# Two layers of a hybrid token mixer with mixture of experts: first norm of layer 1 inside the combination, second norms with paired squares, experts' order written before the row lists

## The reference

```
for l in range(2):
    hx = rms_norm(x, norm1_g[l]) * (1 + scx1) + shx1        # first norm; context likewise
    ... px = hx @ w_in[l]; three mixers ...
    x = x + gx1 * merge_branches(...)
    h2 = rms_norm(x, norm2_g[l]) * (1 + scx2) + shx2        # second norm
    x = x + gx2 * moe_ffn(h2, router, experts, shared)
# rms_norm(z, g) = z * rsqrt(mean(z*z) + 1e-6) * g
# moe_ffn: scores = sigmoid(h @ w_router); the 8 best experts of the 4 best groups of 8;
#   y = 2.5 * sum over them of gate * (silu(h@Wg[e]) * (h@Wu[e])) @ Wd[e]  +  shared(h)
```

## Time and profile before

| | |
|---|---|
| three runs, us | 2924.26, 2929.12, 2937.09; median 2929.12 |
| the profiled execution, us | 2925.09 |
| its span, us | 2923.3 |
| TensorE's mean granted clock (1 is full) | 0.929 |
| busy: TensorE, its weight loads, VectorE, ScalarE, GpSimd | 85%, 56%, 44%, 27%, 16% |
| moved by DMA | 462 MB |

### The profile page before, as it was taken

One profiled execution on the slowest core, in us unless ns is written; L12 is line 12 of the kernel. 1 busy time (PEld: TensorE's weight loads), 2 busy tenths in 40 slices (PEclk: granted clock), 3 DMA queues, 4 the chain that ended last, 5 costly groups with the idle time before them and its releaser, 6 DMA issues. The chain is left out here.

```text
span 2923.3 us, 50391 instructions
## 1 busy us (share of the span) xinstructions
PE 2487.6 (85%) x20460; PEld 1627.9 (56%) x20460; DVE 1282.5 (44%) x2785; ACT 800.9 (27%) x1915; POOL 479.5 (16%) x530
## 2 busy tenths in 40 slices
PE   6999889588879997899898599988678879797976
PEld 3444455277744444466665455557367768664544
DVE  4877664787741013532222600054767741422213
ACT  2111264554430002122222101053445430121211
POOL 0000000244430001032232000000235420122220
PEclk8999999699989997999999799989699989899998
DMA  8646101000023201599895723113000033299885
GB/s 339 244 187 246 71 31 44 30 4 3 3 106 138 110 0 49 228 388 350 338 353 213 316 87 115 58 60 116 1 3 3 3 147 135 86 420 367 354 347 230
DMA packets 73831, 462.03 MB, mean 158 GB/s; under 512 B 19072, under 2 KB 26368, under 8 KB 44416
## 3 DMA queue, kind: packets, MB, share of 16 engines
q1 hardware_dynamic: 46848, 408.42, 35.4%
q0 software_dynamic: 26752, 50.39, 4.6%
HBM read 441.95 MB, written 62.91 MB: 173 GB/s over the span
## 5 line engine op out<-in xcount | busy, mean ns | idle before, releaser
L501 PE MATMUL win_ps<-h,win_ring 128*128 128x512 f32 (+1 forms) x1024 | 398.0, 550 | 18.6 <-PEq L377 13.2
L2315 PE MATMUL xp_psG<-moe_ring,rt_xt 128*64 128x256 f32 (+1 forms) x2048 | 351.8, 396 | 5.1 <-DMA moe_ring<-in_moe 4.8
L501 PEld LDWEIGHTS win_ps<-h,win_ring 128*128 128x128 f32 x1024 | 196.1, 193 | 211.9 <-issue 205.0
L2315 PEld LDWEIGHTS xp_psG<-moe_ring,rt_xt 128*64 128x64 f32 (+1 forms) x2048 | 255.8, 167 | 76.1 <-issue 19.1
L561 DVE SCALAR_TENSOR_TENSOR mod_acc<-ada_ring,cv_silu,mod_acc 128x512 f32<-128x512 f32 x280 | 198.0, 748 | 10.8 <-issue 0.4
L2336 PE MATMUL xp_psY<-moe_ring,rt_aT 128*64 128x512 f32 (+1 forms) x512 | 178.6, 606 | 13.8 <-DVE rt_aT L2587 13.8
L2198 POOL DMA_INDIRECT y_rows<-rt_y,rt_dst x92 | 92.3, 1004 | 495.7 <-DVE rt_y L2592 250.1
L1931 PE MATMUL mg_psG<-h,mg_ring 128*128 128x512 f32 (+1 forms) x480 | 166.7, 507 | 0.0
L2580 DVE TENSOR_TENSOR rt_sg<-rt_sg,xp_psG 128x128 f32<-128x128 f32 x92 | 26.4, 287 | 288.8 <-ACT rt_sg L2387 288.8
L1734 PE MATMUL sc_ps<-sc_NT,sc_XI 64*64 64x64 f32 x2560 | 149.0, 220 | 1.0
L2300 PEld LDWEIGHTS xp_psT<-cst,rt_xg 128*128 128x128 f32 x736 | 85.0, 145 | 111.5 <-DMA rt_xg<-h_rows,rt_tok 73.0
(11 more groups left out here) (448 smaller groups left out, 4199.2 us busy)
## 6 DMA issues: line engine op xcount, KB each, us to landing
moe_ring<-in_moe SPq DMA_DIRECT2D x128, 1536.0 KB, 13.0
ada_ring<-in_ada SPq DMA_DIRECT2D x22, 2048.0 KB, 14.9
win_ring<-in_win SPq DMA_DIRECT2D x20, 2048.0 KB, 7.8
cb_yg<-y_rows SPq DMA_DIRECT2D x24, 1024.0 KB, 15.5
mg_ring<-in_mg SPq DMA_DIRECT2D x10, 1536.0 KB, 7.7
mg_ring<-in_mg SPq DMA_DIRECT2D x16, 768.0 KB, 4.4
ml_gate_ring<-in_mg SPq DMA_DIRECT2D x18, 512.0 KB, 3.6
mg_wo<-in_wo SPq DMA_DIRECT2D x2, 4096.0 KB, 16.4
```

The lines of the kernel that those rows point to most:

```text
L501: last = pe.matmul(ps[:, n % NB, first(n):T], ring[:, j % 2, c, m * P:(m + 1) * P], h[:, c, first(n):T], start=c == 0, stop=c == KD - 1)
L2315: last = pe.matmul(psG[at:at + m, u % 2, 0:2 * P].rearrange("p (q n) -> p q n", q=2), xt[:, u % 2, c, at:at + m], ring[:, slot, c:2 * KD:K ...
```

## The change

1. **Second norms.** VectorE adds the squares in pairs, so that TensorE sums four tiles and not eight. The inverse root is exp(-0.5 ln(.)), both on ScalarE, with no reciprocal. VectorE makes scale and shift of the last two channel tiles itself. SP loads the router's weights here, in the stage ahead of the one that uses them.
2. **First norm of layer 1.** It is no longer a stage. stage_combine of layer 0 runs inside layer 1's frame and norms each tile of 128 tokens behind its residual: one square over 1024 columns, sums, logarithm, exponential, one multiplication over 1024 columns, eight modulations of 128. Half of the slots of `cb_yg` lie in `pr`. The projection's first weights are loaded behind the last rows, and `x` is written in two parts.
3. **Experts' order.** TensorE computes it behind 6 (layer 0) or 8 (layer 1) of the shared expert's first products, and VectorE writes `perm` and `passes` before the eight rounds of the row lists.

```diff
-def stage_norm(nc, k, l, which, x, h, t0, x_home=None):
-
-    sq_done, sum_done, root_done, scaled, h_done, x_saved = k.signals(
-        "norm_sq", "norm_sum", "norm_root", "norm_scaled", "norm_h", "norm_x_saved")
+def stage_norm(nc, k, l, x, h, t0, wr):
+
+    sq_done, pair_done, sum_done, logged, root_done, scaled, h_done = k.signals(
+        "norm_sq", "norm_pair", "norm_sum", "norm_log", "norm_root", "norm_scaled", "norm_h")
     N = T - t0
-    shift, scale = (0, 1) if which == 1 else (3, 4)
...
+
+            @block.sync
+            def _(sp):
+                sp.dma_start(wr[:], k.d_rt[l].rearrange("p (c n) -> p c n", n=E_ROUTED)).then_inc(k.wr_in.sem, 16)
...
                 act.wait_ge(sum_done.sem, sum_done.at(1))
-                act.activation(rstd[:, t0:T], ps[:, 0:N], ACT.Sqrt, scale=1.0 / D, bias=k.cst("eps")[:, 0:1]
-                               ).then_inc(root_done.sem, 1)
...
-                for c in range(KD):
+                act.activation(rstd[:, t0:T], ps[:, 0:N], ACT.Ln, scale=1.0 / D, bias=k.cst("eps")[:, 0:1]
+                               ).then_inc(logged.sem, 1)
+                act.wait_ge(logged.sem, logged.at(1))
+                act.activation(rstd[:, t0:T], rstd[:, t0:T], ACT.Exp, scale=-0.5).then_inc(root_done.sem, 1)
+                for c in range(KD - BY_DVE):
                     act.wait_ge(scaled.sem, scaled.at(c + 1))
-                    for s in range(2):
-                        if s * CTX >= t0:
-                            last = act.activation(h[:, c, s * CTX:(s + 1) * CTX], tmp[:, c, s * CTX:(s + 1) * CTX],
-                                                  ACT.Identity,
-                                                  scale=k.mod[:, l, s, scale * KD + c:scale * KD + c + 1],
-                                                  bias=k.mod[:, l, s, shift * KD + c:shift * KD + c + 1])
+                    for out, src, scale, shift in parts(c):
+                        last = act.activation(out, src, ACT.Identity, scale=scale, bias=shift)
                     last.then_inc(h_done.sem, 1)
...
             def _(dve):
+                for c in range(0, KD, 2):
+                    dve.wait_ge(sq_done.sem, sq_done.at(c + 2))
+                    dve.tensor_tensor(tmp[:, c, t0:T], tmp[:, c, t0:T], tmp[:, c + 1, t0:T], ALU.add
+                                      ).then_inc(pair_done.sem, 1)
                 dve.wait_ge(root_done.sem, root_done.at(1))
-                dve.reciprocal(rstd[:, t0:T], rstd[:, t0:T])
-                dve.drain()
...
+                dve.drain()
+                for c in range(KD - BY_DVE, KD):
+                    for out, src, scale, shift in parts(c):
+                        last = dve.tensor_scalar(out, src, scale, shift, ALU.mult, ALU.add)
+                    last.then_inc(h_done.sem, 1)
 
             @block.tensor
             def _(pe):
-                for c in range(KD):
-                    pe.wait_ge(sq_done.sem, sq_done.at(c + 1))
-                    last = pe.matmul(ps[:, 0:N], k.cst("ones"), tmp[:, c, t0:T], start=c == 0, stop=c == KD - 1)
+                for c in range(0, KD, 2):
+                    pe.wait_ge(pair_done.sem, pair_done.at(c // 2 + 1))
+                    last = pe.matmul(ps[:, 0:N], k.cst("ones"), tmp[:, c, t0:T], start=c == 0, stop=c == KD - 2)
                 last.then_inc(sum_done.sem, 1)
...
-                sp.dma_start(wr[:], k.d_rt[l].rearrange("p (c n) -> p c n", n=NE)).then_inc(wr_in.sem, 16)
                 sp.dma_start(sw, k.d_moe[l, E_ROUTED:E_ALL].rearrange("a p (c n) -> p a c n", n=P)
                              ).then_inc(sw_in.sem, 16)
...
-                for c in range(4, KD):
+                for c in range(4, KD if l else 6):
+                    shared_in(0, 0, c)
+                pe.wait_ge(ordered.sem, ordered.at(1))
+                pe.matmul(psOrder[:, 0:NE], eid[:], oh[0:NE], start=True, stop=True)
+                pe.matmul(psOrder[:, NE:NE + 4], k.cst("ones", NE)[:, 0:1], over[:], start=True, stop=True
+                          ).then_inc(order_ps.sem, 1)
+                for c in range(KD if l else 6, KD):
                     shared_in(0, 0, c)
                 for c in range(KD):
                     last = shared_in(0, 1, c)
                 last.then_inc(gu_done.sem, 1)
-                pe.wait_ge(ordered.sem, ordered.at(1))
-                pe.matmul(psOrder[:, 0:NE], eid[:], oh[0:NE], start=True, stop=True)
-                pe.matmul(psOrder[:, NE:NE + 4], k.cst("ones", NE)[:, 0:1], over[:], start=True, stop=True
-                          ).then_inc(order_ps.sem, 1)
...
                 windowed(1)
-                for j in range(HALF // 8):
-                    last = eight(j)
-                last.then_inc(listed.sem, 1)
...
+
+                for j in range(HALF // 8):
+                    last = eight(j)
+                last.then_inc(listed.sem, 1)
...
+
+            low = pr[:].rearrange("p a n -> p (a n)").rearrange("p (s j n) -> p s j n", j=PER, n=D)
+            yg += [low[:, j] for j in range(SL - own)]
+            sq = ctx.enter_context(nc.sbuf_tensor(f"cn_sq{l}", [P, 2, KD, P], F32))
+            tmp = ctx.enter_context(nc.sbuf_tensor(f"cn_tmp{l}", [P, 2, KD, P], F32))
+            rstd = ctx.enter_context(nc.sbuf_tensor(f"cn_rstd{l}", [P, 2, P], F32))
+            psN = ctx.enter_context(nc.psum_tensor(f"cn_ps{l}", [P, 2, 512], F32))
...
+                    sp.dma_start(yg[m % SL], d_y[m // NG, m % NG]).then_inc(y_in[m % SL].sem, 16)
+                if norm:
+                    load_projection(sp, k, l + 1, 0)
+                    load_projection(sp, k, l + 1, 1)
+                    for i, (a, b) in enumerate(((0, NTT - 1), (NTT - 1, NTT))):
+                        sp.wait_ge(x_done.sem, x_done.at(b))
+                        sp.dma_start(k.d_x[:, :, a * P:b * P], x[:, :, a * P:b * P]).then_inc(x_saved.sem, 16)
+                        sp.wait_ge(x_saved.sem, x_saved.at(16 * i + 16))
...
+                    def square(tt):
+                        act.wait_ge(x_done.sem, x_done.at(tt + 1))
+                        act.activation(sq[:, tt % 2], x[:, :, tt * P:(tt + 1) * P], ACT.Square).then_inc(sq_done.sem, 1)
+
+                    def root(tt):
+                        act.wait_ge(sum_done.sem, sum_done.at(tt + 1))
+                        act.activation(rstd[:, tt % 2], psN[:, tt % 2, 0:P], ACT.Ln, scale=1.0 / D,
+                                       bias=k.cst("eps")[:, 0:1]).then_inc(logged.sem, 1)
+                        act.wait_ge(logged.sem, logged.at(tt + 1))
+                        act.activation(rstd[:, tt % 2], rstd[:, tt % 2], ACT.Exp, scale=-0.5).then_inc(root_done.sem, 1)
+
+                    def modulate(tt):
+                        act.wait_ge(scaled.sem, scaled.at(tt + 1))
+                        s = tt * P // CTX
+                        for c in range(KD):
+                            last = act.activation(h[:, c, tt * P:(tt + 1) * P], tmp[:, tt % 2, c], ACT.Identity,
+                                                  scale=k.mod[:, l + 1, s, KD + c:KD + c + 1],
+                                                  bias=k.mod[:, l + 1, s, c:c + 1])
+                        last.then_inc(h_done.sem, 1)
+
+                    square(0)
+                    for tt in range(1, NTT):
+                        root(tt - 1)
+                        square(tt)
+                        modulate(tt - 1)
+                    root(NTT - 1)
+                    modulate(NTT - 1)
+
             @block.vector
             def _(dve):
+                def normalise(tt):
+                    dve.wait_ge(root_done.sem, root_done.at(tt + 1))
+                    if tt >= 2:
+                        dve.wait_ge(h_done.sem, h_done.at(tt - 1))
+                    dve.tensor_tensor(tmp[:, tt % 2], x[:, :, tt * P:(tt + 1) * P],
+                                      rstd[:, tt % 2].unsqueeze(1).broadcast_to([P, KD, P]), ALU.mult
+                                      ).then_inc(scaled.sem, 1)
...
+                    if norm and tt >= 2:
+                        dve.wait_ge(x_done.sem, x_done.at(tt - 1))
+                        normalise(tt - 2)
                 residual(NTT - 1)
+                if norm:
+                    normalise(NTT - 2)
+                    dve.wait_ge(x_done.sem, x_done.at(NTT))
+                    normalise(NTT - 1)
 
...
+                def square_sum(tt):
+                    pe.wait_ge(sq_done.sem, sq_done.at(tt + 1))
+                    if tt >= 2:
+                        pe.wait_ge(root_done.sem, root_done.at(tt - 1))
+                    for c in range(KD):
+                        last = pe.matmul(psN[:, tt % 2, 0:P], k.cst("ones"), sq[:, tt % 2, c], start=c == 0, stop=c == KD - 1)
+                    last.then_inc(sum_done.sem, 1)
+
...
+                    if norm and tt:
+                        square_sum(tt - 1)
+                if norm:
+                    square_sum(NTT - 1)
...
```

(11 more changed lines are left out.)

72 lines of the change are left out of this document (36 added, 36 removed).

## The result

| | before | changed |
|---|---|---|
| median of the runs, us | 2929.8 (4 runs, 2924.26 to 2937.09) | 2905.06 (4 runs, 2903.99 to 2909.11) |
| profiled execution: time, span, us | 2925.09, 2923.3 | 2905.49, 2903.7 |
| TensorE's mean granted clock | 0.929 | 0.932 |

The ratio is 0.9917, with a 95% interval from 0.9893 to 0.9941. The median of before is 2929.8 here, with a fourth run, and was 2929.12 when I predicted. 2906 was predicted. The two ranges of whole times don't touch, but the difference is under 1%, so what each part gave is read from stretches of the profiles.

What follows compares the result with a forecast made beforehand. Bound by one-engine chains at the norms and TensorE's waits for router's weights, gathered rows and experts' weights. 4.3 + 1.4 + 5.4 + 5.0 + 7.0 = 23.1 us off 2925.1 gives 2902.0, predicted median 2906, range 2891 to 2918.

Steps and rivals of the forecast that it cites:

- Second norms: Chain from squares to modulations in both layers' second norms: shorter by 4.3 us in layer 0, 1.4 in layer 1.
- Rival (d): Every ScalarE table load costs 1.38 us of drain beyond its 1.28, 8.3 us in all: 2914; chance 0.05.
- Router's weights: Start of the scores: loading one stage ahead removes TensorE's wait, 2.7 us in each layer, 5.4 in all.
- The collision with the clearing: Layer 1: GpSimd's gather-buffer clearing over VectorE's first steps could take at worst 1.3 us of the gain; nothing was charged.
- First norm of layer 1: Norm inside layer 0's combination: the projection starts at 1677.5 for 1682.5, gain 5.0 us.
- 17 to 18: Sign: us from the last residual to ScalarE's last modulation before the projection, with eight table loads in the combination.
- Rival (c): The combination's tail is longer, modulations at 0.50 and residual later: 3 to 4 us less gain, 2910; chance 0.11.
- Order ahead: Expert loops: pass count before the row lists, first weights 11.8 and 7.8 us earlier; gains 2 and 5 us taken.
- rival (f): The order is not ahead because TensorE's two small products come late; called small and counted in (a).
- Rival (b): The expert loops are bound by bytes and give back the whole head start: 8 us more, 2898; chance 0.12.
- Rival (a): The expert loops keep their stalls, set by gathers and stores: only 16.1 us gained, 2913; chance 0.23.
- Rival (e): Earlier weights delay the first gathers in the DMA queues; 49 us of waiting for rows double: 2962; chance 0.04.

Runs made afterwards that it cites:

- e8: Changed kernel with square root and reciprocal, not logarithm and exponential, for the tiles' norm inside the combination; 2899.5 us median of 5 runs, ratio 0.9910.
- e5: Changed kernel with the router's weights loaded back at the head of the mixture's stage; 2902.59 us, one run.
- e7: Changed kernel with square root and reciprocal again in the second norms, pairs and VectorE's modulations kept; 2904.33 us, one run.
- e12: Changed kernel with the router's weights loaded late in the mixture's stage, the same kernel executed once more; 2916.78 us, one run.
- e6: Changed kernel with layer 1's first norm again a stage of its own behind the combination; 2910.19 us median of 10 runs, ratio 0.9931.
- e2: Changed kernel with SP holding the first expert's load until TensorE has ended the shared expert's last product; 2928.09 us, one run.
- e9: Changed kernel with layer 0's combination tail reordered, square roots for tiles 2 and 3, four of their eight modulations on VectorE; 2897.73 us median of 6 runs, ratio 0.9891.

## Why the prediction was right

**Second norms.** The mechanism and the order of events came out as forecast. In layer 0 the sum was late: the logarithm starts at 1137.87, 7.55 us after the first square, where I had 6.95, because half clock took more of it than the 1.0 that I had charged (in e8, with the sum at full clock, its end is 6.17 us after the first square, for 5.95). Over all kernels with the changed norm it is 16.0 to 18.5 us to the scores, and 23.8 to 25.6 without: the means, 17.2 (eight profiles, without e5, e7 and e12) and 24.5 (three), are 7.3 apart, for 7.0 forecast. In layer 1 the even trade between the reciprocal and the second load is shown by e7.

**Rival (d), a drain behind each table load,** falls. In the rows of the combination the logarithm starts 1.30 us after its load starts (1654.95, 1656.25), and the 1.29 to 1.30 us repeat at all eight loads but the first, behind which the logarithm waits for TensorE's sum. The loads themselves start 0.01 to 0.02 us behind the instruction before them. The Trainium skill, ScalarE: Activation LUTs, section What ACT_TABLE_LOAD costs, has 1.38 us of draining beside the 1.28; neither here nor in the earlier trace rows is there any sign of it.

**Router's weights.** 2.3 to 3.2 us in layer 1, as forecast. In layer 0 the wait at the scores is removed as forecast, but only 1.7 of 2.7 us can be found at the pass count, with a spread as large as that. The collision with the clearing that I left uncharged did not happen: in layer 1 the two-input operation at 2512.16 and the maxima behind it lie under the clearing (2507.41 to 2513.53), and take 0.36 and 1.19 us, what they took before outside it. That agrees with the Trainium skill, SBUF — State Buffer, section Who interferes with whom, by which a two-input VectorE instruction is not held up by a GpSimd instruction that only writes SBUF.

**First norm of layer 1.** 5.4 measured by the profiles and 5.8 by e6, for 5.0. From the last residual to the end of ScalarE's last modulation it is 16.8 us (1670.56 less 1653.77). That is what my own chain adds up to (1677.2 less 1660.4); the "17 to 18" among the signs was written down wrongly. The delay of the last residual was 0.5 to 1.2 us, for 1.1. A modulation of 128 columns took 0.40 (3.19 for eight), which is the 0.39 that I had by the slope between 512 and 256 columns. Rival (c) falls.

**Order ahead.** The pass count comes 11.9 and 7.6 us earlier behind the first score, for 11.8 and 7.8, so rival (f) falls. The price in layer 1 was 5 and is 5.9 (6.5 by the two profiles). The reason given, that the head start reaches the first stalls and not the gathers, is what the waits show in layer 1: those for weights went, those for rows stayed. The sign "waits for gathered rows smaller in sum" came out by 1.6 and 1.4 us, within what a kernel differs from itself; the sign "the first stall later" came out in layer 0 (79.6 us behind the first turn before, 91.0 and 92.5 in the two profiles of the changed kernel). Rival (b), which gave back the whole head start (8 us), falls by e2: 24 us of head start are worth 10.6. Rival (a) falls in layer 1. In layer 0 the 2 us are neither shown nor refuted: that the profiles gave 1.8 is luck. Rival (e) did not come: rows are waited for 25.1 and 20.7 us, not twice as long.

The errors of the terms are small: 0.5 us too much was forecast for layer 0's norm, 0.4 too little for the combination, 1.5 too little for layer 1's loop. The price of that loop had been chosen between two bounds (0 and 15 for both loops) and not worked out, so its nearness is in part luck. The rest of the span had 4.7 us against me in the profile, and the median came to 2905.06. That it is within 1 us of the forecast is luck as well, with whole times that range over 5 us for this kernel and 13 for the one before.

## What to carry to other kernels

Where only one engine works at a time between two stages, price the chain from its own rows: what leaves it leaves the whole time, and before such a chain is called done, look at what stands ahead of its last link on each engine (here e9's new order, with other roots for two tiles and eight modulations on VectorE, gave 8.4 us, where moving the norm into the stage had given 5.4). Count an earlier start of weights at what the engine waits for weights and little more, not at its length (10 us more of head start gave 5.9, and 4.5 to 5.9 was the wait). A start that is too late can also come back as another wait: in layer 0 of e2 more than half of the loss was waiting for rows. If an effect is below the scatter of whole runs, cut the traces at the same events, compare the stretches, and repeat a kernel to learn how well each of them repeats.

## What the runs showed of the hardware that I had not expected

The same eight passes over 512 columns took 4.25, 5.58 and 6.62 us to their end in three kernels, behind the same work, with a granted clock of 1.00, 0.69 and 0.55 over them, and a sum so short moves the chain behind it by up to 2.4 us. And a program's untouched stages, with the same instructions, were 1981.5 us in one execution and 1997.2 in another. The granted clock of the whole hardly seems to move, from 0.925 to 0.932 in all the profiles, but over 2900 us such a step is 20 us of TensorE's time: in the rest of the two profiles of the kernel before it is 32 us more at half clock, beside 13.2 us more of time. ScalarE's Square and Identity between two square roots needed no table load (e8 has one load in the combination where the changed kernel has eight).
